# Two chained mixer blocks on one core: a different schedule for the opening, with two projection blocks run between the w_ada units

## What is computed

```
mod   = silu(c) @ w_ada + b_ada            # 2048 x 6144; same weights for c_ctx
shift, scale, gate = split(mod, 3)
h  = rmsnorm(x,   g_pre) * (1 + scale)   + shift      # x:   512 x 2048
hc = rmsnorm(ctx, g_pre) * (1 + scale_c) + shift_c    # ctx: 256 x 2048
z  = h @ w_in      # 2048 x 12352; columns 0:4096 are x, B, C of a Mamba scan ("xbc")
zc = hc @ w_in[:, :4160]
xbc = silu(depthwise_conv5(z[:, :4096]))
```

## Time and profile before

| | us |
|---|---|
| median of 3 runs (2937.72 to 2942.34) | 2938.05 |
| the profiled execution | 2930.63 |
| its span, first to last instruction | 2928.8 |
| TensorE busy (98% of the span) | 2870.9 |
| VectorE busy | 1463.3 |
| ScalarE busy | 977.6 |
| GpSimd busy | 378.4 |

### The profile page before, as it was taken

One profiled execution on the slowest core, in us unless ns is written; L12 is line 12 of the kernel. 1 busy time (PEld: TensorE's weight loads), 2 busy tenths in 40 slices (PEclk: granted clock), 3 DMA queues, 4 the chain that ended last, 5 costly groups with the idle time before them and its releaser, 6 DMA issues. The chain is left out here.

```text
span 2928.8 us, 37143 instructions
## 1 busy us (share of the span) xinstructions
PE 2870.9 (98%) x15238; PEld 2388.2 (82%) x15238; DVE 1463.3 (50%) x1736; ACT 977.6 (33%) x1317; POOL 378.4 (13%) x436
## 2 busy tenths in 40 slices
PE   7899999999999999999999999899999999999999
PEld 3288888888789997888788888688888888888787
DVE  3776777744555456676652333523333344324533
ACT  4522322234343333343332332323343343222311
POOL 2211000100334124322310000100000000000000
PEclk9999999999999999999999999899999999999999
DMA  8666766644455554555455433232222222322342
GB/s 323 254 251 239 262 245 241 229 158 132 142 162 165 157 172 141 155 170 177 144 180 185 135 104 94 108 108 74 70 86 66 80 75 84 99 82 93 113 153 94
DMA packets 162136, 439.61 MB, mean 150 GB/s; under 512 B 14768, under 2 KB 59824, under 8 KB 151728
## 3 DMA queue, kind: packets, MB, share of 16 engines
q1 hardware_dynamic: 122928, 304.13, 32.0%
q0 software_dynamic: 16224, 96.13, 9.2%
q10 hardware_dynamic: 22816, 36.97, 3.6%
HBM read 398.11 MB, written 39.06 MB: 149 GB/s over the span
## 5 line engine op out<-in xcount | busy, mean ns | idle before, releaser
L1404 DVE TENSOR_TENSOR WL<-RAW,WH 128x1024 fp32r<-128x1024 f32 x424 | 524.0, 1245 | 857.8 <-ACT WH L896 645.5
L432 PE MATMUL PB<-HH,WH 128*128 128x512 f32 x2048 | 818.4, 400 | 0.0
L437 PE MATMUL PB<-HL,WH 128*128 128x512 f32 x2048 | 803.1, 392 | 0.0
L438 PE MATMUL PB<-HH,WL 128*128 128x512 f32 x2048 | 802.6, 392 | 0.0
L896 ACT ACTIVATE WH<-RAW 128x1024 fp32r<-128x1024 f32 x424 | 438.4, 1054 | 441.2 <-PE PB L472 208.9
L432 PEld LDWEIGHTS PB<-HH,WH 128*128 128x128 f32 x2048 | 386.1, 189 | 86.6 <-issue 7.1
L438 PEld LDWEIGHTS PB<-HH,WL 128*128 128x128 f32 x2048 | 386.0, 188 | 66.8
L437 PEld LDWEIGHTS PB<-HL,WH 128*128 128x128 f32 x2048 | 386.6, 189 | 65.4 <-issue 3.1
L470 PE MATMUL PB<-WH,HH 128*128 128x512 f32 x768 | 299.5, 390 | 2.9 <-DVE evb L1404 1.4
L472 PE MATMUL PB<-WH,HL 128*128 128x512 f32 x768 | 298.8, 389 | 0.0
L471 PE MATMUL PB<-WL,HH 128*128 128x512 f32 x768 | 298.8, 389 | 0.0
(11 more groups left out here) (270 smaller groups left out, 3196.1 us busy)
## 6 DMA issues: line engine op xcount, KB each, us to landing
RAW<-in_w_in_t SPq DMA_DIRECT2D x320, 512.0 KB, 3.7
AU<-in_w_ada POOLq DMA_DIRECT2D x64, 1024.0 KB, 5.5
RAW<-in_w_out_t SPq DMA_DIRECT2D x96, 512.0 KB, 3.6
aus<-in_w_ada_s SPq DMA_DIRECT2D x36, 512.0 KB, 14.0
bcb<-R SPq DMA_DIRECT2D x64, 256.0 KB, 6.2
S<-so ACTq DMA_DIRECT2D x24, 384.0 KB, 2.7
xs<-in_w_ada_s SPq DMA_DIRECT2D x16, 512.0 KB, 8.9
ebc<-R SPq DMA_DIRECT2D x32, 256.0 KB, 6.2
```

The source lines that it names most:

```text
L432: h.matmul(banks[j], lh, m.HH[:, t, :], start=st, stop=False)
L437: h.matmul(banks[j], lh, m.HL[:, t, :], start=False, stop=False)
L438: ins = h.matmul(banks[j], ll, m.HH[:, t, :], start=False, stop=en)
L1404: return h.tensor_tensor(o, a, b, op)
```

## The change

- All 64 w_ada units are split; `ADA_WHOLE`, `scd` and the direct float32 matmuls are gone. They use slots 0 to 2 of `WH` and `WL`; slot 3 is for the early blocks.
- The six x and ctx tiles are all kept (`xs`), scaled in place by DVE, and turned by PE transposes of one channel tile at a time straight before it is modulated; `dg`, `XN` and `XC` are gone. ACT forms `hf` from PSUM, in place of DVE and POOL.
- The opening is written in 44 *beats* (`beat`). Beats 0 to 31 hold two w_ada units each. Beats 9 to 37 hold the 16 turns, beats 4, 8, ..., 32 the folds. Beats 12 to 43 each hold one *quarter unit* of xbc (one channel tile of one unit: `t_tile`): block 0 and block 12 take turns, four quarters each.
- The blocks' order becomes 0, 12, 1, ..., 11, 13, 14, 15 (`BLOCKS`), and w_in's tiles are packed in that order on the host. The xbc loops of all engines skip the eight units already done, and with them the `ada_side` steps that stood there.

```diff
+PLACE = list(range(16)) + list(range(16, 24)) + list(range(6, 14)) + \
+    list(range(14, 24)) + [12, 13, 14, 15, 16, 17] + list(range(18, 24)) * 2 + [18, 19, 20, 21]
+BLOCKS = (0, 12) + tuple(range(1, 12)) + (13, 14, 15)
+EARLY = 8
+def beat(k):
+    st = k // 4 - 1 if k % 4 == 0 and 4 <= k <= 32 else None
+    p, r = divmod(k - 9, 8)
+    t = 4 * p + min(r, 3) if k >= 9 and r in (0, 1, 2, 4) and p < 4 else None
+    return st, t, k - 12 if 12 <= k < 12 + 4 * EARLY else None
...
# tensor_program
+    for k in range(BEATS):
+        if k < 32:
+            a_unit(2 * k)
+            a_unit(2 * k + 1)
+        st, t, sub = beat(k)
+        if st is not None:
+            fold(st)
+        if t is not None:
+            turn(t)
+        if sub is not None:
+            u, b, tt, t = early_tile(sub)
+            P.wait_ge(*at("g hi", u, tt // 2))
+            P.wait_ge(*at("g lo", u, tt // 2))
+            first_h(t)
+            tk = early[u % 2]
+            ins = t_tile(m.WH[3][:, tt * 256:(tt + 1) * 256], m.WL[3][:, tt * 256:(tt + 1) * 256], t,
+                         [tk[0][1], tk[1][1]], tk[2][1] if b < 12 else None)
...
# scalar_program
+    for k in range(BEATS):
+        t = beat(k - 1)[1]
+        if t is not None:
+            modulate(t)
+        for i in (2 * k, 2 * k + 1):
+            if i + 2 < 64:
+                a_high(i + 2)
+            if 3 <= i < 15 and i % 2:
+                v = (i - 3) // 2
+                A.wait_ge(*at("x", v))
...
+                junk = A.then(act(m.junk, m.xs[v], ACT.Square, acc=m.ss[:, v:v + 1]), "x squared", v)
+        sub = beat(k + 2)[2]
+        if sub is not None and sub % 2 == 0:
+            early_high(sub)
...
# vector_program
+    for k in range(BEATS):
+        st, t, sub = beat(k - 1)
+        if st is not None:
+            finish(st)
+        if t is not None:
+            h_low(t)
+        for i in (2 * k, 2 * k + 1):
+            if i + 2 < 64:
+                a_low(i + 2)
+            if 5 <= i < 17 and i % 2:
+                v = (i - 5) // 2
+                V.wait_ge(*at("rr", v))
+                V.then(TS(m.xs[v], m.xs[v], m.rr[:, v:v + 1], None, ALU.mult), "xs", v)
+        if beat(k + 1)[0] is not None:
+            rows_out(beat(k + 1)[0])
+        sub = beat(k + 2)[2]
+        if sub is not None and sub % 2 == 0:
+            early_low(sub)
...
# sync_program
+    for i in range(64):
+        if i >= 16 and i % 8 == 0:
+            raw_load(i // 8 - 2)
+        ada_load(i)
+        if i % 2 and i < 12:
+            load(m.xs[i // 2], m.x_tile(I, i // 2), s.x[i // 2], "x", i // 2)
+    for u in range(6, 68):
+        raw_load(u)
```

More of the change, by code:

```diff
@@ new lines, in a_unit @@
+    def a_unit(i):
+        st, kk = divmod(i, 8)
+        bank = reuse(5) if kk == 0 else PB[5]
+        P.wait_ge(*at("scs"))
+        P.wait_ge(*at("a hi", i))
+        P.wait_ge(*at("a lo", i))
+        for j in range(2):
+            for part in (m.WH[i % 3], m.WL[i % 3]):
+                ins = h.matmul(bank[0:4, :], m.scs[:, 2 * kk + j, :], part[:, j * 512:(j + 1) * 512],
+                               start=kk == 0 and j == 0 and part is m.WH[i % 3],
+                               stop=kk == 7 and j == 1 and part is m.WL[i % 3])
+        ins.then_inc(*put(s.unit, "a used", i))
+        freed[5] = [("rowb", st)]
@@ L418, in tensor_program, with turn @@
-    fold(7)
+    def turn(t):
+        P.wait_ge(*at("cst"))
+        for v in range(6):
+            P.wait_ge(*at("xs", v))
+        if t:
+            P.wait_ge(*at("hx", t - 1))
+            P.wait_ge(*at("hc", t - 1))
+        for v in range(4):
+            ins = h.transpose(PB[6][:, v * 128:(v + 1) * 128], m.xs[v][:, t * 128:(t + 1) * 128], ident)
+        ins.then_inc(*put(P.side, "turn", t))
+        P.wait_ge(*at("mod", 2 * (t // 4) + (1 if t % 4 < 3 or t == 15 else 2)))
+        for v in range(2):
+            ins = h.transpose(PB[7][:, v * 128:(v + 1) * 128], m.xs[4 + v][:, t * 128:(t + 1) * 128], ident)
+        ins.then_inc(*put(P.side, "turn ctx", t))
@@ new lines, in tensor_program @@
+    ring = deque(range(6))
+    early = [[take(ring, "xbc", b, j) for j in range(3 if b < 12 else 2)] for b in BLOCKS[:2]]
+    for k in range(BEATS):
[15 more added lines that the diff above has]
+                         [tk[0][1], tk[1][1]], tk[2][1] if b < 12 else None)
+            if tt % 2:
+                ins.then_inc(*put(s.unit, "g used", u, tt // 2))
@@ L1504, in vector_program @@
[L1504 to L1516 removed]
+        t = V.then(TT(m.modv[:, c:c + 4, :], sums[:, :, 0:2],
+                      m.P("b_ada", c, 4).unsqueeze(2).to_broadcast([128, 4, 2]), ALU.add))
+        V.wait_ge(*t)
+        t = V.then(TT(m.modv[:, c:c + 4, :], m.modv[:, c:c + 4, :], sums[:, :, 2:4], ALU.add), "mod", st)
@@ L1517, in vector_program @@
+    make(8)
+    make(9)
+    for e in ("turn", 15), ("turn ctx", 15), ("HL", 15), ("CL", 15), ("fold", 7):
+        V.wait_ge(*at(*e))
     for i in range(2):
@@ L2485, in tables @@
     put("fold", np.tile(np.eye(64), (2, 1)))
-    put("fold4", np.tile(np.eye(2), (2, 1)))
     half = 64
```

521 lines of the change are left out of this document (196 added, 325 removed).

## The result

Over four runs each, alternating on one chip, the changed kernel takes 2926.3 us (median; 2921.27 to 2927.6) and the kernel before 2940.2 (2937.72 to 2942.42): ratio 0.995, 95% interval 0.9933 to 0.9967. It is faster by 13.9 us, where 29 were forecast. Two later comparisons on other chips gave 0.9966 (0.9953 to 0.9978) and 0.996 (0.9945 to 0.9974), gains of 9.9 and 12.2 us. The sign was right. 2926.3 lies outside the stated range, which ended at 2925, by 1.3 us: that range was counted from 2938.05, the median then known, and the gain of 13.9 itself lies just inside its lower bound of 13. The two later gains lie outside it.

The account below looks back on a forecast made before the run. No engine bounds the opening, a chain of turns between them; PE is full afterwards. 67.6 until full + 103.7 full beats + 8.3 waits = 179.6 against 208.7, a gain of 29.1: forecast 2909 us, range 2893 to 2925.

Parts of the forecast that it names:

- Until PE is full: Opening up to beat 12: loads, w_ada halves, first turn and modulations were to let beat 12 start at 67.6 us.
- The trap in SP's queue: Opening: the first w_in load waits for the last ctx square; DMA stands still from 39.6 to 44.8, unit 16 at 50.1.
- Full beats: From beat 12 PE has work in every beat: w_ada units, quarter units, turns and folds, together 103.7 us.
- The debt of two convolutions: Block 1: DVE's convolutions of blocks 0 and 12 delay unit 10's low half, 3.2 us more of waiting.
- none is bunched: Xbc loop: the 76 needed `ada_side` steps fit into 66 + 4 + 4 before block 15 and two in it.
- At nothing: `w_dt`: Before the dt product: `w_dt`, issued in block 15's second unit, is ready some 2 us early and costs nothing.
- A: Opening's turns: transposes cost what the old turns did, 18.5 us instead of 8.1, giving 2919; chance 0.08.
- B: Opening's beats: DVE sets the beat as low halves stretch, 8 to 14 us go, 2917 to 2923; chance 0.17.
- C: Opening: a quicker start, DMA hardly stops, beat 12 near 60, giving 2901; chance 0.12.
- E: Opening's beats: engines in lockstep without overlap, 7.3 us instead of 4.0 per beat with a turn, 2962; chance 0.04.
- F: Opening: early blocks save nothing, beats lose what quarter units cost, within 0.2% of 2938; chance 0.03.
- D: Xbc stage: gain given back, 8 to 12 us rather than 3, giving 2915 to 2920; chance 0.10.

Follow-up runs that it names:

- rows: Changed kernel with DVE's copy of a stripe's row sums moved ahead of the beat's second low half: 2917.26 us in one run.
- fill: Changed kernel plus eight unused matmuls on PE between the last early quarter unit and block 1: 2925.07 us in one run.
- the second profile: The changed kernel run again without any edit, on another chip: 2925.73 us, ratio 0.9966 to the kernel before.
- late: Changed kernel with unit 54's halves made ahead of the convolution of block 11, on ACT and DVE: 2926.18 us in one run.
- mid: Changed kernel with unit 54's low half made on DVE between the two halves of block 11's convolution: 2917.28 us in one run.
- notrain: Changed kernel with each train of one-column matmuls replaced by one matmul, so values differ: 2881.12 us.
- thin: Changed kernel with the one-column matmuls spread, two ahead of each half channel tile of the next unit: 2948.47 us, ratio 1.0045 to the kernel before.
- zero: Changed kernel with DVE's four memsets of zp and zc moved two beats earlier: 2913.96 us in one run.
- all: Changed kernel with five moves (units 10 and 11, memsets, first w_in tile, row copy, one accumulation): 2910.38 us, ratio 0.9897 to the kernel before.
- four: Changed kernel with four moves (units 10 and 11, memsets, first w_in tile, row copy): 2905.07 us, ratio 0.989 to the kernel before.
- five: The kernel of four plus unit 54's low half between the halves of block 11's convolution: 2906.85 us, ratio 0.9899 to the kernel before.

## Why the prediction was wrong

The profiled execution misses the sum by 19.8 us. By the steps of the prediction:

- **Until PE is full: 4.1 (67.6 became 71.66).** The trap in SP's queue was right to half a microsecond. The step that failed is "Turn 0 needs unit 19 used: 57.6"; it came at 60.56. For this PE needed the copy of the row sums at 54.38, which DVE had behind two low halves and a scaling, and the w_ada matmuls from 55.10 on ran at 1.2 GHz (0.63 us a record) until 57.6. In *rows*, where the copy stands further ahead, turn 0 comes at 58.89, 1.7 sooner, with the same half clock; the rest of the 3.0 is that clock. The other 1.1 lies between turn 0 and beat 12, where ACT started 0.6 behind the turn and its modulations took 1.95 each (65.56 to 67.51), not 1.7; *rows* gains it back by the second copy.
- **Full beats: 2.7.** The forecast was 108.8 from beat 12 to block 1 (103.7, 4 of waits, 1.1), measured 111.5. 1.6 is the half clock behind the 3.12 us of idle time at 71.66, 0.7 the handover (1.82 instead of 1.1). The rest nearly cancels: the other waits were 2.4 (1.10, 1.10 and 0.23) where 4 were allowed, and the work took 2 us more than 103.7. Eight beats lasted 33.97 from 107.21 to 141.18, 32.87 without their wait, where 32.1 were counted. The durations of single steps came close to what was priced (0.62 and 0.41 for these two). Six transposes took 0.66, the fold 0.34:

```profile
60.56 0.60 PE L440 MATMUL PB<-cst,xs 128*128 128x128 f32 x4
60.99 0.38 PE L444 MATMUL PB<-cst,xs 128*128 128x128 f32 x2
61.22 0.39 PE L415 MATMUL PB<-WH,scs 128*4 128x512 f32 x1
```

- **The debt of two convolutions: 2.2.** Unit 10 was forecast 20.1 after block 1's start, 3.2 late; it came 20.5 after, 3.6 late. The size was right. Missing was the half clock behind the wait, up to 1.7.
- **The xbc stage past block 1: 6.1.** 1.6 is a longer fall at the first train: the two blocks that hold trains last 40.42 and 37.28, those of the kernel before 37.29 and 38.83. Some 4 is block 13, a wait of 2.38 and the half clock behind it, on which the sum had nothing: "After that DVE needs 27 of every 33.8 us, so the debt is gone in a block" is true only as long as blocks last 33.8. And "none is bunched" left out that the skipped `ada_side` steps come due there. Another 0.7 is the price of the work moved up: without ctx a block lasts 21.76 us in the kernel before (616.56 to 638.32), not 22.5.
- **From the dt product to the end: 4.7.** Lost clock is larger, mostly at the trains (from the dt product to the last matmul: 18.8 against 13.7). In the other two profiles of the changed kernel this part is 4.4 and 6.3 longer than in the kernel before, and lost clock 3.4 and 6.8 larger, so the clock covers it to within 1 us each time. How much of it the change causes stays open: there is one profile of the kernel before, and with 2930.63 it is among the fastest of that kernel's runs (2928.7 to 2943.68) and has, at 0.992, as high a mean clock as any of them.
- **At nothing: `w_dt`.** Right: PE has no gap at 646.1, with 0.3 us to spare instead of 2.

Together 19.8. Some 12 of them (1.3 at 55, 1.6 at 71.66, 1.7 at 204, 1.6 at the train, 1.7 at 587, 4.7 behind) are granted clock, on which the sum had no term; the others are waits and work. None of the prediction's signs of being wrong came: PE idled some 4 us from 70 to 170, block 1 began before 190, and PE did not wait for `WD`. They watched the opening and `w_dt`, and not the clock or block 13.

The price by the Trainium skill's "DMA: Bandwidth & Descriptors", section Bandwidth, did not come: DMA held 407 to 417 GB/s while nothing blocked it, not near 358. Of TensorE's clock, the Trainium skill's "TensorE: Matmul & The Clock Gate", Terms, prices time at the lower clock as that time multiplied by one less the ratio; the trace comes near (3.4 us at 0.50 are 1.7 by that rule, and the block with such a fall was 1.54 longer).

Of the rivals, A fell (0.107 us between transposes), B and C did not come, and E and F are far off. D is what happened, in part: "DVE's debt of two convolutions, tiles of `AU` that come late and `w_dt` behind block 15" were to cost 8 to 12; from block 1 to the dt product 462.9 us pass, where the kernel before takes 451.4 for the same work (152.4 to 660.1, less the 56.3 moved up). These 11.5 us, of which 3.2 had been counted, are D's cost, though `w_dt` had no share and the clock a large one. D was priced as the only thing to go wrong. With the opening 4 us late as well, the two together come to the edge of the range (a gain of 13.9) and in the later comparisons leave it (9.9 and 12.2); it had been drawn over single cases, and they were independent.

## What to carry to other kernels

Give the granted clock a term of its own: a wait of some 2 us on an engine that is otherwise full may cost some 1.6 more behind it, and a train of one-column matmuls can do so with PE busy throughout. Before an idle time of PE is priced, ask who sets the next meeting point: at block 1 it was DVE, and neither filled idle time (*fill*) nor a full clock (the second profile) gained anything. When blocks get shorter, an engine that fitted into a long one has to be summed again over the short ones, and moving its work within them did not help here (*late*, *mid*).

## What the runs showed of the hardware

The granted clock fell to 1.2 GHz for 3.4 us, sometimes 6.8 (412 to 420), in and behind trains of matmuls one column wide, four times in the first profile without any idle time of PE; none of these falls was left when the trains were left out. After an idle time it fell in some executions and not in others. Behind the same 1.80 to 1.82 us ahead of block 1 it did in 4 profiles (the changed kernel's first, *mid*, *notrain*, *thin*) and did not in 7 (its second and third among them). Behind the 3.1 us ahead of beat 12 it did in 9 and did not in 3 (*zero*, *fill*, *mid*). Behind 1.98 or 1.99 us there it did not in *rows* and *all*, and did in *four* and *five*.
